# Weight chunks of half the rows for 512 columns, and memory's tiles split during the gate's last steps

## The reference, cut to what matters

```python
for l in range(2):
    x = x + 0.5 * rms_norm(swiglu(rms_norm(x)))
    h = rms_norm(x)
    proj = h @ w_in        # NSA q, k, v | gates | retention q, k, v, g (4 x 512 columns)
    nsa  = three attention branches over 8 heads (compressed, selected, window)
    ret  = retention over 4 heads; its output is multiplied by silu(g)
    x = x + rms_norm(concat(nsa, ret) @ w_out)
    # memory attention: keys and values from a memory of 256 tokens
    mem = rms_norm(memory) ;  mk, mv = mem @ wk, mem @ wv      # 1024 columns each
    x = x + rms_norm(attention(rms_norm(x) @ wq, mk, mv) @ wo)
    x = x + 0.5 * rms_norm(swiglu(rms_norm(x)))
```

## Time and profile before

| | before |
|---|---|
| time, median of 3 (lowest to highest) | 3209.89 us (3209.39 to 3211.18) |
| profiled execution: its time, its span | 3210.59 us, 3209.3 us |
| TensorE busy, mean granted clock | 3158.3 us (98%), 0.997 |
| DVE, ACT, POOL busy | 1333.6, 1193.6, 1336.7 us |
| DMA | 285.28 MB, mean 89 GB/s |

### The profile page before, as it was taken

One profiled execution on the slowest core, in us unless ns is written; L12 is line 12 of the kernel. 1 busy time (PEld: TensorE's weight loads), 2 busy tenths in 40 slices (PEclk: granted clock), 3 DMA queues, 4 the chain that ended last, 5 costly groups with the idle time before them and its releaser, 6 DMA issues.

```text
span 3209.3 us, 44579 instructions
## 1 busy us (share of the span) xinstructions
PE 3158.3 (98%) x17592; PEld 2701.5 (84%) x17592; DVE 1333.6 (42%) x2571; ACT 1193.6 (37%) x2116; POOL 1336.7 (42%) x865
## 2 busy tenths in 40 slices
PE   8999999999999999999999999999999999999998
PEld 7887888898888988888888889888988898798887
DVE  7675533124330445645353304331155655353311
ACT  5454322233222344554432223322344554443221
POOL 4442444443444343452344444444533254334443
PEclk9999999999999999999999999999999999999999
DMA  4221233332323241231223332333332122123332
GB/s 159 79 66 47 86 105 93 99 111 74 97 89 106 82 133 54 67 102 57 79 79 101 94 95 86 100 101 101 112 107 67 54 86 86 59 73 105 98 98 68
DMA packets 80942, 285.28 MB, mean 89 GB/s; under 512 B 8928, under 2 KB 11360, under 8 KB 80480
## 3 DMA queue, kind: packets, MB, share of 16 engines
q1 hardware_dynamic: 79728, 278.59, 29.1%
q10 hardware_dynamic: 1008, 3.84, 0.3%
HBM read 280.30 MB, written 2.10 MB: 88 GB/s over the span
## 4 chain that ended last, share of the span: by engine, by line
PE 90%; DVE 4%; POOL 2%; ACT 2%; issue 1%; DMA 0%; ACTq 0%; DVEq 0%; POOLq 0%
PE bank L269 22%; PE bank L271 22%; PE bank L270 22%; PE bank L277 4%; PE bank L278 4%; PE bank L279 4%; PE bank L1426 3%; POOL wlo L263 2%; PE bank L1399 2%; PE bank L1411 1%; PE bank L3320 1%; DVE m_xbc L2126 1%; PE bank L3294 1%; PE bank L567 1%; ACT whi L249 1%
## 5 line engine op out<-in xcount | busy, mean ns | idle before, releaser
L263 POOL TENSOR_TENSOR wlo<-raw,whi 128x1024 fp32r<-128x1024 f32 (+3 forms) x775 | 1215.3, 1583 | 1549.5 <-ACT whi L249 1515.4
L269 PE MATMUL bank<-hhi,whi 128*128 128x512 f32 x2080 | 824.8, 397 | 12.6 <-DVE wlo L263 10.9
L270 PE MATMUL bank<-hlo,whi 128*128 128x512 f32 x2110 | 822.2, 390 | 0.0
L271 PE MATMUL bank<-hhi,wlo 128*128 128x512 f32 x2080 | 811.2, 390 | 0.0
L249 ACT ACTIVATE whi<-raw 128x1024 fp32r<-128x1024 f32 (+2 forms) x502 | 500.4, 1030 | 345.2 <-PE bank L271 283.2
L269 PEld LDWEIGHTS bank<-hhi,whi 128*128 128x128 f32 x2080 | 391.3, 188 | 94.3 <-issue 16.3
L270 PEld LDWEIGHTS bank<-hlo,whi 128*128 128x128 f32 x2110 | 397.0, 188 | 81.0 <-issue 1.0
L271 PEld LDWEIGHTS bank<-hhi,wlo 128*128 128x128 f32 x2080 | 390.9, 188 | 83.0
L269 PE MATMUL bank<-ff_ahi,whi 128*128 128x512 f32 x660 | 256.7, 389 | 0.0
L271 PE MATMUL bank<-ff_ahi,wlo 128*128 128x512 f32 x660 | 256.7, 389 | 0.0
L270 PE MATMUL bank<-ff_alo,whi 128*128 128x512 f32 x630 | 245.1, 389 | 0.0
(11 more groups left out here) (430 smaller groups left out, 5608.3 us busy)
## 6 DMA issues: line engine op xcount, KB each, us to landing
raw<-wstream SPq DMA_DIRECT2D x508, 512.0 KB, 3.5
raw<-wstream SPq DMA_DIRECT2D x20, 256.0 KB, 2.6
xa_v<-memT ACTq DMA_DIRECT2D x2, 1024.0 KB, 5.0
outT<-x SPq DMA_DIRECT2D x4, 512.0 KB, 2.8
raw<-wstream SPq DMA_DIRECT2D x4, 420.0 KB, 4.4
x<-xT ACTq DMA_DIRECT2D x2, 512.0 KB, 7.8
x<-xT SPq DMA_DIRECT2D x2, 512.0 KB, 8.0
consts<-consts SPq DMA_DIRECT2D x1, 1004.0 KB, 6.7
```

The costliest lines, as they stand in the source:

```text
L263: last = g.tensor_tensor(h.lo[:, o:o + step], h.raw[:, o:o + step], h.hi[:, o:o + step].bitcast(F32), ALU.subtract)
L269: t.matmul(out, l[0], r[0], start=start, stop=False)
L270: t.matmul(out, l[0], r[1], start=False, stop=False)
L271: return t.matmul(out, l[1], r[0], start=False, stop=stop)
```

## The change

Weights that move (z, v, retention's v and gate, memory's values) come in chunks of 512 columns for 512 rows, two such chunks (a pair) for a product. A matmul then moves 512 columns and fills a whole bank. A pair's products are accumulated over both chunks: with `together=4` (first layer) all four token blocks with the first chunk, then all with the second; with `together=2` (second layers) two token blocks with the first chunk, the same two with the second, and then the other two. The number of beats stays (a beat is 3 matmuls of 512 columns instead of 6 of 256). ACT and DVE handle 512 columns at once, half as often, and the one tile for `tanh` is used whole. In the second layers the three empty beats are gone on every engine; ACT splits memory's tiles in the gate's beats 24 to 31 (counted from 0 within the pair), DVE one beat behind; `xa_mlo` and `nsa_lo` change places so that only tiles of the first chunk's rows are overwritten.

```diff
+def pe_moving_wide(k, pair, acts, width=T, together=TB):
+    t = k.nc.tensor
+    for t0 in range(0, width // P, together):
+        for part, ch in enumerate(pair):
+            for tb in range(t0, t0 + together):
+                if ch.free[tb] is not None:
+                    t.wait_ge(*ch.free[tb])
+                for kk in range(4):
+                    if tb == 0:
+                        pe_half_begin(k, ch, kk)
+                    o = (4 * part + kk) * width + tb * P
+                    last = mm3(k, k.bank[ch.banks[tb]][:, :], [x[:, o:o + P] for x in acts], ch.weights(kk, 0, T), part + kk == 0, part * kk == 3)
+                    pe_step_end(ch, last, kk, kk == 3, tb == len(ch.banks) - 1)
+                    yield
...
+def wide_pair(k, banks, evac, together=None):
...
+    return [Chunk(k, banks, evac, nk=4, pitch=T, done=places[0]), Chunk(k, banks, first=False, nk=4, pitch=T, done=places[1])]
...
+def pair_apart(k, pair, steps):
+    c = pair[0].c
+    for n, _ in enumerate(steps):
+        if n == 2:
+            weight_hi(k, c + 1, 1)
+        if n == 23:
+            weight_hi(k, c + 2, 0)
+        if n == 25:
+            weight_hi(k, c + 2, 1)
+        yield
+    weight_hi(k, c + 3, 0)
+
+def pair_pool(k, pair):
+    yield from beats(23)
+    weight_lo(k, pair[0].c + 2, pieces=4)
+    yield from beats(9)
+    weight_lo(k, pair[0].c + 3, pieces=4)
...
         for ch in self.rch:
             yield from pe_stationary(k, ch, part, KT)
-        for ch in self.vrch + self.grch:
-            yield from pe_moving(k, ch, h, 0, 256)
-        yield from beats(3)
+        for pair in (self.vrch, self.grch):
+            yield from pe_moving_wide(k, pair, h, together=2)
...
-        for ch in self.mvch:
-            yield from pe_moving(k, ch, m, 0, 256, width=MEM)
+        for pair in self.mvch:
+            yield from pe_moving_wide(k, pair, m, width=MEM, together=2)
...
+        gate = silu_tokens_act(k, self.grch[1], self.gr_used, self.gr_tanh, k.tmp[0], k.r_tok_half, 12)
+        for n, _ in enumerate(gate):
             if n == 2:
-                weight_hi(k, ch.c + 1, 1)
+                weight_hi(k, self.grch[1].c, 1)
+            if n == 24:
+                a.wait_ge(*self.grch[0].done[-1])
+            if n >= 24:
+                self.act_split(n - 24)
+            if n in (25, 27):
+                weight_hi(k, self.mkch[0].c, (n - 25) // 2)
             yield
...
+        for n, _ in enumerate(silu_tokens_dve(k, self.grch[1], self.gr_used, self.gr_tanh, k.tmp[0], self.gr, 12)):
+            if n >= 25:
+                self.dve_split(n - 25)
             yield
```

More of the change, by code:

```diff
@@ L1639, in both_apart, with keep_tokens_act @@
     weight_hi(k, ch.c + 2, 0)
-def keep_tokens_act(k, ch, dst, kept, n=256, root=None, then=True, ready=None):
+def keep_tokens_act(k, ch, dst, kept, root, before=4, ready=None):
     a = k.nc.scalar
     for tb, b in enumerate(ch.banks):
-        yield from beats(KT // 2)
+        yield from beats(before if tb % 2 == 0 else 4)
         a.wait_ge(*ch.done[tb])
@@ L1676, in beside, with two_items @@
         run(steps)
+def two_items(steps):
+    return [itertools.islice(steps, 16), steps]
 def shifted(items, lag):
@@ L1810, in pe @@
         last.then_inc(self.dt_done.sem)
-        dense = [pe_moving(k, ch, h, 0, 256) for ch in self.zch]
+        dense = two_items(pe_moving_wide(k, self.zch, h))
         for c in range(2):
@@ L1860, in act @@
         a.wait_ge(*self.h.half[0])
-        dense = [self.act_z(c, ch) for c, ch in enumerate(self.zch)]
+        dense = [idle_act(k, self.zch[0], 16), self.act_z(self.zch[1])]
         for c in range(2):
@@ L2854, in act_filler @@
+        yield from beats(2)
+        weight_hi(k, self.mkch[1].c, 0)
+        yield from beats(2)
+        weight_hi(k, self.mkch[1].c, 1)
+        yield from beats(3)
+        yield from idle_act(k, self.mkch[0], 1)
         for ch in self.mkch[1:]:
             yield from idle_act(k, ch, 8)
-        for c, ch in enumerate(self.mvch):
-            yield from keep_tokens_act(k, ch, lambda tb: self.mem_v[:, tb * D + c * 256:tb * D + (c + 1) * 256], self.mv_kept, root=self.m_rs, then=c < 3)
+        for c, (first, ch) in enumerate(self.mvch):
+            yield from idle_act(k, first, 8)
+            yield from keep_tokens_act(k, ch, lambda tb: self.mem_v[:, tb * D + c * T:tb * D + (c + 1) * T], self.mv_kept, self.m_rs)
+            if c == 0:
+                weight_hi(k, ch.c + 2)
@@ L3039, in pool_filler @@
         k = self.k
-        for ch in self.rch + self.vrch + self.grch:
+        for ch in self.rch:
             yield from idle_pool(k, ch, 16)
-        yield from beats(3)
-        for ch in self.mkch + self.mvch[0:3]:
+        for pair in (self.vrch, self.grch):
+            yield from pair_pool(k, pair)
+        for ch in self.mkch + self.mvch[0] + self.mvch[1][0:1]:
             yield from idle_pool(k, ch, 8)
@@ L3537, in cols, with pairs @@
         pad(t.reshape(P, nk * 256))
+    def pairs(w, c0):
+        for k0 in (0, 4):
+            pad(w[k0 * P:(k0 + 4) * P, c0:c0 + T].reshape(4, P, T).transpose(1, 0, 2).reshape(P, 4 * T))
     def wide(w):
@@ L3556, in lay_out @@
         cols(w, c)
-    for c in (1536, 1792, 3080, 3592, 3336, 3848, 0, 256, 512, 768, 1024, 1280):
+    pairs(w, 1536)
+    for c in (3080, 3592, 3336, 3848, 0, 256, 512, 768):
         cols(w, c)
+    pairs(w, 1024)
     for pair in range(4):
@@ L3575, in lay_out @@
         wide(w[:, np.r_[VALUES, 1280:1304]])
-        for c in range(1304, 3352, 256):
+        for c in range(1304, 2328, 256):
             cols(w, c)
+        for c in (2328, 2840):
+            pairs(w, c)
         for n in ("xa_wk_2", "xa_wv_2", "w_out_2", "xa_wq_2", "xa_wo_2"):
+            if n == "xa_wv_2":
+                for c in (0, T):
+                    pairs(a[n][l], c)
+                continue
             for pair in range(4):
```

139 lines of the change are left out of this document (56 added, 83 removed).

## The result

| | before | changed |
|---|---|---|
| time, median of 20 runs each (lowest to highest) | 3209.99 us (3208.89 to 3213.93) | 3215.51 us (3212.75 to 3216.32) |
| profiled execution: its time, its span | 3210.59 us, 3209.3 us | 3216.32 us, 3215.0 us |
| TensorE busy, mean granted clock | 3158.3 us, 0.997 | 3152.8 us, 0.995 |
| matmuls | 17592 | 16824 |

The changed kernel takes 1.0015 times as long (95% interval 1.0009 to 1.0022): 5.5 us more, inside the band of 0.2% that I called "no change", but 5.5 us above the top of my range (3210) and 9.5 above my number (3206).

What follows compares the result with a forecast made beforehand. TensorE, busy 98% of the span, was taken to bound the kernel. Terms -10.3 + 2.5 - 0.15 (first layer) + 3.4 + 0.5 = -4.05 us took 3210.59 to 3206.5, as a median 3206; range 3198.5 to 3210.

Steps and rivals of the forecast that it cites:

- The dense products: On TensorE, 1536 narrow matmuls with weights moving become 768 wide ones at 0.2265 us from start to start: -10.3 us.
- The slower restart: Dense blocks that follow attention start slowly, wide ones losing about 0.05 us more each: +2.5 us.
- The stops at the keys: TensorE's stops in each second layer, at the keys and the end: 7.0 us against 5.3, +3.4 us in all.
- bank 7: First key product waits for the gate's last read, queued behind attention on ACT and DVE: 5.6 us, bounds 2.4 to 6.5.
- `xa_k`: Second key chunk's wait for bank 6, behind DVE's operations and copy after retention's transposes: 0.9 us a layer, not 1.9.
- the end: After attention's last transposes the filler is gone, so TensorE waits for copies the last output needs: 0.5 us a layer.
- The clock: After the longer stop, at least the old dip of TensorE's clock, one chance in three of another: +0.5 us (-1.7 to +1.7).
- The moved beats themselves are the same work: In the second layers, moving the beats adds no cost of its own; no term in the sum.
- nothing else is late after it: After the stop for the gate's last read, ACT and DVE catch up while TensorE does keys and attention; no further loss.
- Hidden, at no cost: Weights for the gate's second chunk, made at 5.7 and 8.5 us, are ready before TensorE needs them at 9.1 and 10.5.
- DVE is not late: Rival: the gate's last read comes as early as inputs allow, stop 2.4 us; total 3199.0 or 3197.5 us; 28 in 100.
- POOL's low parts come late: Rival: TensorE stops four times for weights of retention's v and gate, 3 us each; about 3218 us; 10 in 100.

Runs made afterwards that it cites:

- Experiment 7: The kernel before with wide chunks in the first layer alone (z and v): 3207.54 us against 3209.78 beside it, ratio 0.9994.
- experiments 3: The changed kernel with memory's weights from the third key chunk on made three beats later on ACT and POOL: 3215.21 us, ratio to before 1.0013.
- experiment 6: The kernel of experiment 5 with memory's value weights moved away from retention's gate steps on ACT and POOL: 3196.46 us, ratio to before 0.9956.
- experiments 10: The changed kernel with only memory's value weights moved away from retention's gate steps: 3211.12 us, ratio to before 1.0003.
- Experiment 1: The changed kernel with the three empty beats put back and memory's tiles split in them, all chunks still wide: 3209.39 us, ratio to before 0.9996.
- second kernel of experiment 9: The kernel of experiment 1 with both halves of the first keys' weights made in the gate's beats 22 and 25: 3203.93 us, ratio to before 0.9979.
- experiment 8: The kernel of experiment 1 with the second half of the first keys' weights behind bank 6's `tanh` on ACT: 3209.24 us, ratio to before 0.9997.
- experiment 2: The changed kernel with the gate's last `tanh` and product one beat earlier, ahead of attention, on ACT and DVE: 3203.70 us, ratio to before 0.9978.
- experiment 5: The kernel of experiment 2 with the second half of the first keys' weights behind bank 6's `tanh` on ACT: 3201.51 us, ratio to before 0.9974.

## Why the prediction was wrong

**The dense products** (-10.3 us) were right: 0.2267 us from start to start, 768 wide matmuls. Experiment 7 is in line with them, though its interval is as wide as the effect. The Trainium skill (TensorE: Matmul & The Clock Gate, Back-to-back issue gap) gives a fixed 2.5 ns for each matmul; by it the first layer would have gained 0.5 us, and it gained 2.6. The same section calls that formula the gap of an isolated matmul and gives about 131 ns for 512 columns in a stream of weight loads and matmuls; the rows here show 226.7, so they agree with neither.

**The slower restart** (+2.5) was of the right kind. A block of 12 wide matmuls behind attention goes from 1291.68 to 1294.51, 2.83 us against 2.72 at the steady pace: 0.11, near the 0.13 that I had. Still the second layers gained 4.5 at most instead of 5.2; where the rest is I have no row for.

**The stops at the keys** (7.0 us a layer): the place, the chain and its names were right. 6.4 us instead of 5.6 at bank 7, inside the bounds given (to 6.5), 0.95 at `xa_k` for 0.9, 0.35 at the end for 0.5.

**The clock** (+0.5, with "one chance in three" for a second dip) was mis-sized: +3.4 us behind the stops. I had priced a dip as one stretch of 3.4 us. After stops of 6.4 us the low clock lasted 10.2 and 6.8 us, of which 6.25 and 4.04 fell on work. That a dip elsewhere (1.7) is absent is no merit of the change that I can show; without this luck the miss would be larger.

**The step that failed** is "The moved beats themselves are the same work", together with "nothing else is late after it": the late steps of retention stood in the sum at nothing and measured 5.5 us, more than any other error. The paragraph on weights asked only whether the low parts of v and gate would be ready for the PE ("Hidden, at no cost"), and about memory's weights it asked nothing. Ready they all were: the PE's waits for `wlo` stayed at 4.7 us (4.8 before). I did not ask what these pieces do to DVE at their new place, though I had the row for it: a split of 0.41 us takes 0.83 beside POOL, and I used it for the splits alone. For the PE the moved beats were the same work, but they slid POOL's work three beats against retention's steps, and the 5.5 us of stops for `m_qr`, `att_s` and `m_otok` came from that (experiments 3, 6 and 10: 4.5 to 5.5 us of these waits go when only the weights are moved; where the PE doesn't have to wait for the weights instead, in experiments 10 and 6, 4.4 and 5.0 us of time come back). The edits move ACT's `weight_hi` along with POOL's pieces, but it is not what slows DVE: in the kernel of experiment 6 six splits with a half of weights on ACT beside them and no piece of POOL take 0.48 us each, and 0.45 to 0.48 alone.

The same effect is in the wide chunks. With half of the rows in a chunk, the gate's first chunk is in use up to its beat 24, and the first keys' weights can only be made in the last beats of the gate, just where ACT's `tanh` and DVE's chain have no slack. Experiment 1 shows the price with the splits back in their old place (a gain of 0.8 us where 7.3 were expected, part of it, 2.8 us in the profiled executions, by the clock), the second kernel of experiment 9 gives it back by two or three beats' difference (6.4), and experiment 8 shows that it has two parts: ahead of the `tanh` the half holds up ACT, behind it POOL holds up DVE.

**The rivals.** "DVE is not late" was wrong as long as the order stands; experiment 2 made it nearly true and came to 3203.7. "POOL's low parts come late" didn't happen; the loss came through DVE. It was the rival nearest to what happened: POOL's weights do decide, by another victim.

## What to carry to other kernels

When beats are taken out of a schedule, ask for each engine what it will run beside after the shift, and not only whether its result comes in time: here 5.5 us were lost between two engines that were both under half busy. Such losses add up with those at a bank or a buffer, and each can be looked for by moving one piece of work by a few beats. And a stop of TensorE of some microseconds has a second price, the work that follows at half the clock: 2 to 3 us for a stop of 6.4 here, and none for stops of 1.5 in experiment 5, though the kernel before lost 1.7 behind stops of up to 2 us in one of its two layers.

## What the runs showed of the hardware

**DVE beside POOL.** With POOL's pieces (0.75 us each) beside them, DVE's steps on 128x128 elements with two SBUF inputs (the gate step) take 0.64 us from start to start instead of 0.29, and those with one input (the centring, `TENSOR_SCALAR`) 0.70 instead of 0.22. Attention's scores, which read a bank (0.68), and the sum over 512 columns (L3222, 0.67) don't change. The Trainium skill (SBUF — State Buffer, Who interferes with whom) says that DVE and GpSimd share a pair of ports as an exclusive lock, which operations with two SBUF inputs and those of the two-port modes need and reductions don't, and that the loser waits for the whole instruction. The rows agree: a step takes about as long as one of POOL's pieces, not twice its own time, and the sums are untouched. In which mode the centring runs no row here shows.

**The clock after a stop.** In the kernels of this study the low clock at the keys of the first of the two layers lasted 10.2 us with a stop of 6.4 us (the changed kernel), 3.4 us with one of 2 us (experiment 2), and was absent with one of 1.5 us (5 and 6). It begins within the stop or just behind it. The same stop of 6.4 us gave 6.8 us in the second of the layers, and in both layers in experiments 3 and 10; the same stop of 2 us gave none in the second layer of experiment 2. So the length of a stop decides only in part, and what else does is open.
